# A new slot table for an expert-gather stage: spacing of query blocks, size of the routing units, ring sizes, one table load

## What is computed

```python
def block_fn(hb):                                    # 128 tokens
    q = (hb @ w_q).reshape(128, 8, 2, 128)           # 8 heads, two half queries each
    s = einsum('thpd,phkd->thpk', q, sub_keys)       # 128 keys a half
    s1, i1 = top_k(s[:, :, 0], 16)
    s2, i2 = top_k(s[:, :, 1], 16)
    cand = s1[..., :, None] + s2[..., None, :]       # 256 candidates a head
    top_s, top_pos = top_k(cand, 16)                 # 16 experts a head
    e = take_along_axis(i1 * 128 + i2, top_pos)
    g = softmax(top_s)
    act = gelu(einsum('thkd,td->thk', u_tab[e], hb))
    return einsum('thk,thkd->td', g * act, v_tab[e])
```

## Time and profile before

| | us |
|---|---|
| median of 3 runs | 1123.68 (1121.61 to 1124.11) |
| the profiled execution, its own time | 1124.39 |
| its span | 1122.6 |
| PE, DVE, ACT, POOL busy | 967.1, 718.2, 395.2, 302.4 |
| DMA | 380.05 MB, mean 339 GB/s |

### The profile page before, as it was taken

How to read it: one execution, slowest core, us unless ns; L and a number is a source line. 1 busy time by engine, 2 the same in 40 slices (tenths; PEclk the granted TensorE clock), 3 DMA queues, 4 the chain that set the end, 5 groups by cost and what they waited for, 6 DMA issues and landing times.

```text
span 1122.6 us, 11227 instructions
## 1 busy us (share of the span) xinstructions
PE 967.1 (86%) x3350; PEld 495.4 (44%) x3350; DVE 718.2 (64%) x1753; ACT 395.2 (35%) x1134; POOL 302.4 (27%) x330
## 2 busy tenths in 40 slices
PE   4898888999999899999998877777887778877777
PEld 2357766676677655555453222222222222222222
DVE  1267475888645887486888888886544445544544
ACT  2111232213502445344455344344333333333332
POOL 0301001002000233334443333343333333333330
PEclk9998999999999999999999999999999999999999
DMA  9950313668246799999999999999999999999994
GB/s 367 361 206 37 156 75 132 263 248 330 88 162 252 290 386 380 415 416 416 419 419 420 419 420 420 421 420 420 419 420 420 420 420 421 419 420 420 419 420 165
DMA packets 51217, 380.05 MB, mean 339 GB/s; under 512 B 5859, under 2 KB 6035, under 8 KB 9814
## 3 DMA queue, kind: packets, MB, share of 16 engines
q0 software_dynamic: 44736, 312.90, 68.3%
q1 hardware_dynamic: 6134, 66.10, 15.0%
q10 hardware_dynamic: 288, 0.35, 0.1%
HBM read 377.74 MB, written 1.59 MB: 338 GB/s over the span
## 4 chain that ended last, share of the span: by engine, by line
PE 45%; DMA 41%; DVE 7%; ACT 4%; issue 2%; SPq 0%; POOL 0%; DVEq 0%; ACTq 0%; POOLq 0%
DMA big<-peer_uv,oT 33%; PE twoA L575 8%; PE twoD L948 8%; PE twoD L950 7%; DMA r<-peer_uv,oT 6%; PE twoA L888 5%; PE twoD L829 3%; DMA big<-weight_rows 2%; PE twoA L553 2%; DVE big L1824 2%; PE twoD L817 2%; PE twoA L497 1%; PE twoA L729 1%; ACT big L1278 1%; PE twoA L703 1%
## 5 line engine op out<-in xcount | busy, mean ns | idle before, releaser
L1057 POOL DMA_INDIRECT big<-peer_uv,oT x259 | 245.5, 948 | 492.5 <-PE twoD L950 369.8
L948 PE MATMUL twoD<-big 128*128 128x512 f32 x518 | 284.5, 631 | 103.6 <-ACT big L1278 100.6
L1824 DVE CUSTOM_DVE_ANT_0 big<-big,twoA 128x1024 f32<-128x1024 f32 x145 | 177.1, 1221 | 166.3 <-DMA big<-peer_uv,oT 166.0
L950 PE MATMUL twoD<-big 128*128 128x512 f32 x518 | 265.4, 594 | 0.0
L948 PEld LDWEIGHTS twoD<-big 128*128 128x128 f32 x518 | 82.6, 189 | 279.8 <-ACT big L1278 246.7
L1273 ACT ACTIVATE oT<-oT 128x1 f32<-128x1 f32 x288 | 58.1, 202 | 353.1 <-DVE oT L1824 349.9
L1824 DVE CUSTOM_DVE_ANT_0 big<-big,twoD 128x1024 f32<-128x1024 f32 x114 | 139.0, 1219 | 55.6 <-DMA big<-peer_uv,oT 53.5
L950 PEld LDWEIGHTS twoD<-big 128*128 128x128 f32 x518 | 98.7, 191 | 124.5 <-issue 124.5
L1278 ACT ACTIVATE big<-ctab,oT 128x128 f32<-128x128 f32 x288 | 115.6, 401 | 9.4
L575 PE MATMUL twoA<-hT,big 128*128 128x288 f32 x448 | 116.5, 417 | 0.0
L575 PEld LDWEIGHTS twoA<-hT,big 128*128 128x128 f32 x448 | 85.5, 195 | 28.4 <-issue 5.9
(11 more groups left out here) (335 smaller groups left out, 934.6 us busy)
## 6 DMA issues: line engine op xcount, KB each, us to landing
big<-weight_rows SPq DMA_DIRECT2D x24, 2048.0 KB, 8.9
big<-weight_rows SPq DMA_DIRECT2D x8, 1024.0 KB, 6.8
big<-peer_uv,oT POOLq DMA_INDIRECT x259, 22.4
r<-weight_rows SPq DMA_DIRECT2D x1, 2048.0 KB, 13.4
big<-weight_rows SPq DMA_DIRECT2D x1, 1312.0 KB, 15.2
xT<-token_rows SPq DMA_DIRECT2D x1, 1152.0 KB, 7.8
out_y_prompt<-r SPq DMA_DIRECT2D x2, 512.0 KB, 8.0
ctab<-consts SPq DMA_DIRECT2D x1, 480.5 KB, 18.2
```

Source lines behind the costliest of these rows:

```text
L948: pe.matmul(acc[0][:, :], diag[j % NDG], row[:, 0:512], start=(s == 0), stop=(s == SLOTS[t] - 1), skip_group_check=True)
L950: mm = pe.matmul(acc[1][:, :], diag[j % NDG], row[:, 512:D], start=(s == 0), stop=(s == SLOTS[t] - 1), skip_group_check=True)
L1057: pool.indirect_dma_start(pairs[home[i]], None, peer_uv, bass.IndirectOffsetOnAxis(ap=eidx[:, t, s:s + 1], axis=0)).then_inc(row_in[home[i ...
L1824: dve.tensor_tensor_reduce(out=row, in0=row, in1=h2tok[t][:, :], scale=1.0, scalar=0.0, op0=ALU.mult, op1=ALU.add, accum_out=dots[:, t, s: ...
```

## The change

Five edits to the tables, and the code that follows from them:

- Block 4 is made before slot 0, as the fifth of `BLOCKS_FIRST`; ACT copies it behind the weights of slot 0. Blocks 5 to 15 stand at slots 4, 10, 16, ... 64. Before, blocks 4 to 15 stood at 1, 4, 9, 13, 18 and then every fifth slot up to 53.
- The first tile's eight heads are eight units of one head. Before, heads 0 to 3 were single and heads 4 to 7 two units of two. Their scores stand at slots 5, 17, 29, 41, 53 and 65 (before 5, 14, 34, 54). The units of tile 0 from the fifth on get one step a slot, the second to fourth two.
- `LATE` runs from slot 67 (before 57), and the rest of the token rows is turned at slot 100 (before 90).
- The ring has 7 buffers up to slot 49, 9 from slot 50 and 11 from slot 74. Before it had 7 up to slot 57 and 11 from 58.
- ACT loads the gelu table behind `exps(0)`, before the copies of blocks 0 and 1. Before, the load came with the first gelu.

```diff
-        NEAR_ROWS, ALL_ROWS, MORE_FROM = 7, 11, 58
+        ALL_ROWS, RING = 11, ((0, 7), (50, 9), (74, 11))
...
-        units = [(0, h, 1) for h in range(4)] + [(t, h, 2) for t in range(3) for h in range(0, SLOTS[t] // HEAD, 2) if (t, h) > (0, 2)]
+        units = [(0, h, 1) for h in range(PH)] + [(t, h, 2) for t in range(1, 3) for h in range(0, SLOTS[t] // HEAD, 2)]
...
-        BLOCKS_FIRST = (2, 3, 0, 1)
-        BLOCK_AT = {1: 4, 4: 5, 9: 6, 13: 7, 18: 8, 23: 9, 28: 10, 33: 11, 38: 12, 43: 13, 48: 14, 53: 15}
-        SCORE_AT = {5: 2, 14: 3, 34: 4, 54: 5}
-        LATE = list(range(57, 57 + 2 * 15, 2))
-        H2_COPY, H2_REST = 60, 90
+        BLOCKS_FIRST = (2, 3, 0, 1, 4)
+        BLOCK_AT = {4 + 6 * n: 5 + n for n in range(11)}
+        SCORE_AT = {5 + 12 * n: 2 + n for n in range(6)}
+        LATE = list(range(67, 67 + 2 * 15, 2))
+        H2_COPY, H2_REST = 60, 100
...
-            while unit < len(units) and i >= SCORED[unit] and n < (2 if units[unit][2] == 1 else 1):
+            while unit < len(units) and i >= SCORED[unit] and n < (2 if unit < 4 else 1):
...
-            n = NEAR_ROWS if i < MORE_FROM else ALL_ROWS
+            n = [rows for first, rows in RING if first <= i][-1]
...
-            for j in BLOCKS_FIRST:
+            for j in BLOCKS_FIRST[:-1]:
                 copy_query(j, P if j < 2 else 0, TOK)
                 if j == 3:
                     copy_scores()
                     exps(0)
+                    L.tell(act.activation(nmax[:, 0:1], ident[:, 0:1], ACT.Gelu_apprx_tanh))
...
                 weigh(j)
+                if j == 0:
+                    copy_query(BLOCKS_FIRST[-1], 0, TOK)
```

More of the change, by code:

```diff
@@ L435, in layer_program @@
         SUB_ORDER = (0, 2, 1, 3)
-        BLOCKS_FIRST = (2, 3, 0, 1)
-        BLOCK_AT = {1: 4, 4: 5, 9: 6, 13: 7, 18: 8, 23: 9, 28: 10, 33: 11, 38: 12, 43: 13, 48: 14, 53: 15}
-        SCORE_AT = {5: 2, 14: 3, 34: 4, 54: 5}
-        LATE = list(range(57, 57 + 2 * 15, 2))
-        H2_COPY, H2_REST = 60, 90
+        BLOCKS_FIRST = (2, 3, 0, 1, 4)
[3 more added lines that the diff above has]
+        H2_COPY, H2_REST = 60, 100
         ROUTE_STEPS = 16
-        SCORED = [0, 0] + [next(j for j, n in SCORE_AT.items() if n == unit) + 2 for unit in (2, 3, 4, 5)] + [LATE[k] + 2 for k in range(4, 9)]
+        SCORED = [0, 0] + [j + 2 for j in SCORE_AT] + [LATE[k] + 2 for k in range(4, 9)]
         ROUTE_PLAN, ROUTED_AT = [], [0]
@@ L909, in late @@
                 elif k < 8:
-                    score_unit(k + 2)
+                    score_unit(k + 4)
                 elif k == 8:
```

## The result

Before and changed kernel side by side on one chip: 1122.21 us (1120.07 to 1124.11) and 1115.45 us (1113.64 to 1119.67), medians of 8 runs each, ratio 0.9945 with a 95% interval of 0.9927 to 0.9963. Two more comparisons gave 0.9941 [0.9928, 0.9955] and 0.9949 [0.9929, 0.9969]. So the change saves 0.55%, 6.2 us, where 3.3 were forecast and 1117.8 was the range's lower end. Part of the distance is not the gain: the kernel before had a median 1.5 us lower in this comparison than the 1123.68 that the forecast was taken from. The profiled execution took 1118.28 us, its span 1116.5.

What follows compares the result with a forecast made beforehand. PE sets the first third, the gather of row pairs the rest. Recovering 5.3 us of early lateness less 2.0 us of exposed refills gives 3.3 us less: 1120.4 us (-0.29%), range 1117.8 to 1123.9.

Steps and rivals of the forecast that it cites:

- PE's lateness, through the ring, causes the early loss: Up to slot 26: PE's early query blocks delay asks for pair n + 7; 4.9 of the 5.3 us lost.
- The edge of 7.5 to 8.1 us: In the early slots with seven buffers: how far PE may be behind the data's line before a pair comes late.
- Tightest place: Slot 28, a block behind slot 27's table switch: PE 7.5 us behind, 6.5 after a refill; cost 0, at most 0.5.
- After slot 53 nothing changes: From slot 53 to the end: eight refills and the same outputs as before, so the loss of 10.1 us stays.
- The refills that PE's lateness hid: Two DVE instruction refills, near slots 9 and 27, now appear at 1.0 us each, taking 2.0 us off the gain.
- refills stay hidden: Rival for the refills near slots 9 and 27: all 5.3 us come back, 1118.4 us; chance 0.12.
- the other term of the sum: The 5.3 us that the gather's data was late at slot 26 in the profile before, taken as recoverable.
- Gelu table loaded early: 0: Ahead of slot 0: first weight ready 1.3 us sooner, but PE is still in block 4, so worth 0.
- Ring and singles at 0: Ring of 9 from slot 50 costs 0; single heads' later table switches, at slots 79 and 95, cost 0.
- Slower: Rival up to slot 64: PE slots cost more after waits; at 2.0 us each 1127.2 us, deciding from about 1.95; chance 0.05.

Runs made afterwards that it cites:

- the pad on DVE: Changed kernel with four one-column memsets and one wait more on DVE behind each dot of slots 160 to 285; ratio to before 0.9998 [0.9984, 1.0013].

## Why the prediction was right in its mechanism and short in its size

- **PE's lateness, through the ring, causes the early loss.** Right. Slot 26 went from 5.3 us behind to 0.0. The edge of 7.5 to 8.1 us was roughly right: no kernel with PE at 7.8 or less up to slot 30 had a pair later than the refills' 0.5 to 1.2, while a lateness of 8.5 to 8.7 cost 0.1 to 0.4 in three places (slot 9 of two kernels, slot 19 with blocks every fifth) and 1.1 to 1.9 in three others, so the edge isn't known closer than that. One reading under it was wrong. The 0.5 us at slot 11's dot gave the upper end of 8.1 and passed for half a refill, but the changed kernel has the same 0.45, with PE at 6.4 us at slot 4, and in neither does the dot wait for its pair (no bracket; in the kernel before DVE routes up to it). Dot of slot 11 in the changed kernel:

```profile
408.06 1.22 DVE L1827 CUSTOM_DVE_ANT_0 big<-big,twoD 128x1024 f32<-128x1024 f32 x1
```

- **Tightest place.** Right: slot 28 at 6.8 to 7.3 us (forecast at most 7.5), PE waiting before some slots, blocks 14.2 to 16.4 us apart (forecast 14.96). The `exps` at slot 27 put PE 3.6 us behind there, not 4.4, and made it wait 1.81 us. The Trainium skill, in "ScalarE: Activation LUTs", section "What ACT_TABLE_LOAD costs", has a drain of 1.38 us behind each load; by it PE would be 2.8 us later, as estimated. The trace disagrees, as it did before: from one load to the next are 1.5 us again (447.2 to 448.8).
- **After slot 53 nothing changes.** Right in the main: 10.0 us of 10.1 for the pair of profiles, with steps at 55, 81, 103, 120, 140, 161, 183 and 247 (forecast 54, 80, 101, 122, 141, 161, 189, 253) and the two outputs, and the pad on DVE gave the cause of the steps. Over four executions before lost 9.0 to 10.1 there, mean 9.5: the later slot 53 was, the less came behind it. So slot 53 gained 5.8 us in the mean and slot 287 kept 5.3.
- **The refills that PE's lateness hid: the step that failed.** The sum took 2.0 us off the gain for them, one refill near slot 9 and one near 27, shown in full at slot 53. Measured were 0.9 to 1.2: the second shows in full or by half, the first by nothing or half. That is 1.1 of the 2.9 us missed. The rival "refills stay hidden" was half right. Hiding doesn't end when asks are in time: with heads in pairs slot 53 is at 0.0 and 0.2, and neither shows in full. Why the early ones are cheap is open; that the engine that carries them isn't yet the last one fits, but was not shown.
- **Before is worse than the profile it was read from: the other term of the sum.** The 5.3 us at slot 26 came from one execution. Four give 5.3, 5.7, 6.0 and 8.2, mean 6.3, and one has the fall of the clock. At slot 287 the mean is 16.3 and not 15.4. That is 0.9 us of gain that one profile couldn't show; most of it is the execution with the fall, which is 2.0 to 2.9 us above the others. That this one was the luckiest of four is chance.
- **The rest.** 4.4 us (15.4 to 11.0) and 0.9 make the gather's 5.3. The other 0.9 of 6.2 us lies inside the intervals (each 1.5 to 2.2 us to a side) and the scatter ahead of the first ask; it stays open. The 1.5 us by which the base itself was lower are no part of the mechanism.
- **"Gelu table loaded early: 0".** Right for this change, and for the stated reason, block 4. But the price of an edit was asked only in the new order. In the old order it goes with 2 us or more of the same loss. Read in a row, the gather is 739.2 us before, 736.4 with ring, late steps and early load, 735.9 with single heads too, and 733.9 with the blocks. No run has the new blocks alone in the old kernel, so what they would be worth there without the load isn't known.
- **Ring and singles at 0.** Right in the changed kernel: 733.9 against 734.15 without the ring of 9, and nothing that can be measured for the singles.
- **Slower.** Up to slot 64 PE's slots took 1.72 us back to back and 1.82 behind a wait, as the prediction took them, far from 1.95.

## What to carry to other kernels

When a loss comes through an edge (a ring that runs dry at 7.5 us), price edits together against the edge and not one by one: here the table load recovered some 2 us when made alone and nothing beside block 4, since the two cure the same wait. Read such a loss from several executions before you size it, above all where the engine waits ahead of it. And where a gather saturates the DMA, count the instructions of the idle engines too: 504 memsets (624 instructions) that fit into DVE's waits cost as much as the whole change won.

## What the runs showed of the hardware

- 128 instructions more on DVE cost a saturated gather 1.0 us, in one step; 128 on ACT 0.4 to 0.7, and only after some had gone by unseen. Both are one instruction packet of 0.01 MB.
- A refill can cost nothing even in a saturated gather: with blocks every fifth slot, 3.6 us behind at slot 53, those near slots 81 and 103 didn't show at 420 GB/s.
- At the start of the slots, behind a wait of 2.75 us, TensorE's granted clock was 0.57 and 0.58 from 384 to 388 us in two of five executions and 1.00 in three, of programs that are the same up to there; it was 1.00 around slot 0 in all fifteen with 1.5 us of wait or none. The execution of before with the fall was 1.7 to 2.6 us later than the other three at slot 1 and 2.0 to 2.9 at the end.
